# DeltaNet in a hybrid decoder trunk: half of one group's output pieces put off by an iteration, a second operand for two groups, and the late chains' steps laid anew

## The reference, cut to what matters

```python
def gated_deltanet(x, w_in, conv_w, a_log, dt_bias, out_norm_g, w_out):
    proj = x @ w_in                       # q, k, v, z and two gates per head
    qkv = silu(causal_depthwise_conv(qkv, conv_w))
    q, k = l2_normalize(q), l2_normalize(k)
    o = chunk_gated_delta_rule(q, k, v, g, beta)      # 32 heads, chunks of 64 tokens
    o = rms_norm(o, out_norm_g) * silu(z)
    return o @ w_out

def chunk_gated_delta_rule(q, k, v, g, beta):         # per head and chunk
    sol = triangular_solve(l_mat, rhs, lower=True, unit_diagonal=True)
    ...
    v_new = u_c - w_c @ state
    o_c = q_c @ state + a_c @ v_new
```

## Time and profile before

| | us |
|---|---|
| median of 3 runs | 2799.17 (2798.56 to 2801.68) |
| the profiled execution | 2803.94 |
| its span, first to last instruction | 2802.1 |
| TensorE busy | 2739.6 |
| VectorE busy | 2219.6 |
| ScalarE busy | 1648.4 |

### The profile page before, as it was taken

The page is one execution under the profiler, slowest core; times in us unless marked ns, Lnnn a source line. Parts: engine busy times, 40 slices in busy tenths (PEclk is TensorE's granted clock), DMA queues, the critical chain, the costliest instruction groups (busy, mean ns, idle before and its releaser), DMA issues.

```text
span 2802.1 us, 40252 instructions
## 1 busy us (share of the span) xinstructions
PE 2739.6 (98%) x13456; PEld 2282.1 (81%) x13456; DVE 2219.6 (79%) x2727; ACT 1648.4 (59%) x2184; POOL 31.0 (1%) x30
## 2 busy tenths in 40 slices
PE   8999999999988999999999999999999999999998
PEld 6878888888877888888888888888887888888887
DVE  5867877878767788888888876557677888888887
ACT  6766767667665555555555555554555555555554
POOL 0000000000000000000000000000000000000000
PEclk9999999999999999999999999999999999999999
DMA  6534444445433566656666656643345666656664
GB/s 239 181 124 153 159 144 163 156 149 167 158 105 113 166 210 199 198 185 203 198 198 203 198 172 224 222 135 114 106 158 188 207 199 200 199 184 200 198 201 166
DMA packets 135097, 493.23 MB, mean 176 GB/s; under 512 B 15009, under 2 KB 15329, under 8 KB 134625
## 3 DMA queue, kind: packets, MB, share of 16 engines
q1 hardware_dynamic: 133776, 487.82, 52.8%
q10 hardware_dynamic: 1232, 4.23, 0.4%
HBM read 489.86 MB, written 2.13 MB: 176 GB/s over the span
## 4 chain that ended last, share of the span: by engine, by line
PE 65%; issue 29%; DVE 3%; ACT 2%; DMA 1%; POOL 0%; POOLq 0%; DVEq 0%; SPq 0%; ACTq 0%
PE ACC L733 10%; PE ACC L735 10%; PE ACC L734 10%; PE SIDE L943 7%; PE SIDE L944 7%; PE SIDE L945 7%; PE ACC L943 3%; PE ACC L944 3%; PE ACC L945 3%; PE SIDE L741 2%; DVE W_LO L1627 1%; DMA RAW<-stream 1%; PE SIDE L1138 1%; ACT W_HI L1194 0%; ACT WORK L1587 0%
## 5 line engine op out<-in xcount | busy, mean ns | idle before, releaser
L1627 DVE TENSOR_TENSOR W_LO<-RAW,W_HI 128x1024 fp32r<-128x1024 f32 x424 | 511.6, 1222 | 268.9 <-ACT W_HI L1194 265.8
L1194 ACT ACTIVATE W_HI<-RAW 128x1024 fp32r<-128x1024 f32 x424 | 443.3, 1057 | 217.5 <-PE ACC L735 183.8
L1436 ACT ACTIVATE W_HI<-WORK 128x1024 fp32r<-128x1024 f32 x320 | 325.4, 1031 | 345.8 <-PE SIDE L945 232.7
L733 PE MATMUL ACC<-W_HI,X_HI 128*128 128x512 f32 x1216 | 491.2, 404 | 17.7 <-DVE W_LO L1627 17.6
L735 PE MATMUL ACC<-W_HI,X_LO 128*128 128x512 f32 x1216 | 477.6, 393 | 0.0
L734 PE MATMUL ACC<-W_LO,X_HI 128*128 128x512 f32 x1216 | 476.7, 392 | 0.0
L1878 DVE TENSOR_TENSOR W_LO<-WORK,W_HI 128x1024 fp32r<-128x1024 f32 x300 | 364.5, 1221 | 119.0 <-ACT W_HI L1436 116.3
L1436 ACT ACTIVATE W_HI<-RAW 128x1024 fp32r<-128x1024 f32 x328 | 314.8, 980 | 237.0 <-PE ACC L735 141.6
L733 PE MATMUL ACC<-W_HI,A_HI 128*128 128x512 f32 x928 | 370.3, 399 | 0.7 <-issue 0.7
L735 PE MATMUL ACC<-W_HI,A_LO 128*128 128x512 f32 x928 | 362.7, 391 | 0.0
L734 PE MATMUL ACC<-W_LO,A_HI 128*128 128x512 f32 x928 | 362.2, 390 | 0.0
(11 more groups left out here) (363 smaller groups left out, 3798.7 us busy)
## 6 DMA issues: line engine op xcount, KB each, us to landing
RAW<-stream SPq DMA_DIRECT2D x752, 512.0 KB, 4.6
WORK<-stream SPq DMA_DIRECT2D x160, 512.0 KB, 4.8
WORK<-gdn_rows ACTq DMA_DIRECT2D x8, 512.0 KB, 6.2
WORK<-xt SPq DMA_DIRECT2D x4, 512.0 KB, 9.3
H<-x SPq DMA_DIRECT2D x2, 1024.0 KB, 13.6
out<-WORK SPq DMA_DIRECT2D x4, 512.0 KB, 3.5
WORK<-tails SPq DMA_DIRECT2D x2, 512.0 KB, 10.8
WORK<-gfin SPq DMA_DIRECT2D x1, 1024.0 KB, 6.6
```

Source lines behind the costliest of these rows:

```text
L733: nc.tensor.matmul(dst, hi[:, at:at + P], wh, start=first and h % 2 == 0 and q == 0, stop=False)
L1194: nc.scalar.activation(W_HI[:, h % WS, :], raw_piece(h), ACT.Copy).then_inc(hi_ready, 1)
L1436: nc.scalar.activation(dst, src, ACT.Copy).then_inc(hi_ready, 1)
L1627: nc.vector.tensor_tensor(W_LO[:, h % WS, :], raw_piece(h), W_HI[:, h % WS, :].bitcast(f32), SUB).then_inc(lo_ready, 1)
```

## The change

Iteration 6 (`EDGE`) leaves the loop body and is written out with the same steps but its own list of pieces: of group 4's eight out pieces it keeps four, in slots 18, 20, 26 and 28, and z moves to 16, 17, 21, 22, 24, 25, 29 and 30. Slots 19, 23, 27 and 31 are left without a piece. The other four are done as `old4` in iteration 7 in slots 16, 18, 20 and 22, where the four pieces of group 5's out move to 23, 25, 27 and 30 and v becomes eight pieces in a row. In iteration 7 v0, s, ks, v1 and o go to slots 20, 21, 22, 23 and 25, osum and oscale to 25 and 26. In iteration 8 z and the first out pieces move a slot or more ahead, and `LAST_STEPS` puts nearly every step into a slot of its own. Groups 5 and 7 use `B_HI` and `B_LO` in place of group 6, because group 4's `A_HI` and `A_LO` are now read one iteration longer.

```diff
+EDGE = LATE_Z - 1
+OWN = (0, 1, EDGE, LATE_Z, GROUPS, GROUPS + 1)
-PIECES_7 = "qk 0 1 2 3 4 5 6 7 v 8 9 10 11 12 13 14 16 out 18 20 25 30"
-PIECES_8 = "old4 0 1 2 3 z 4 5 6 8 9 10 11 12 out 13 14 15 16 18 19 20 26"
+PIECES_6 = "qk 0 1 2 3 4 5 6 7 v 8 9 10 11 12 13 14 15 z 16 17 21 22 24 25 29 30 out 18 20 26 28"
+PIECES_7 = "qk 0 1 2 3 4 5 6 7 v 8 9 10 11 12 13 14 15 old4 16 18 20 22 out 23 25 27 30"
+PIECES_8 = "old4 0 1 2 3 z 4 5 6 7 8 9 10 11 out 12 13 14 15 16 18 19 26"
@@ def gdn_acc(it, part, n):
-    return ACCS.get((it, part, n), 0) if isinstance(it, int) and it in GDN_PIECES else GDN_ACC.get(part, 0)
+    return ACCS.get((it, part, n), 0) if isinstance(it, int) and it in GDN_PIECES and it != EDGE else GDN_ACC.get(part, 0)
@@ LAST_STEPS = gdn_table(SOLVE, """
-    0 y0 t0 u0 conv_v0a
-    2 y1 t1 u1 conv_v0b
-    3 y2 strict
-    4 t2 u2 conv_v1a
+    0 y0
+    1 t0 u0 conv_v0a
+    2 y1 conv_v0b
+    3 t1 u1
+    4 y2 strict conv_v1a
+    5 t2 u2 conv_v1b
     6 y3
-    7 t3 u3 conv_v1b silu_v
+    7 t3 u3 silu_v
     8 y4
     9 t4 u4
     10 v_t2 y5
     11 t5
     12 u5 nw
     13 ru
-    14 v0 s
-    15 ks
-    16 v1 o
-    18 osum oscale
+    14 v0
+    15 s
+    16 ks
+    17 v1
+    18 o osum
+    19 oscale
     20 o_t""")
@@ SOLVE_7 = gdn_table(SOLVE, """
     18 ru
-    19 v0
-    21 s ks
-    23 v1 fill o
-    24 osum
-    25 oscale
+    20 v0
+    21 s
+    22 ks
+    23 v1 fill
+    25 o osum
+    26 oscale
     30 o_t""")
@@ def gdn_steps(it, hs):
-    table = {0: FIRST_STEPS, 1: SOLVE_1 + PREP_1, LATE_Z: SOLVE_7 + PREP_7, GROUPS: LAST_STEPS,
+    table = {0: FIRST_STEPS, 1: SOLVE_1 + PREP_1, EDGE: SOLVE_STEPS + PREP_STEPS, LATE_Z: SOLVE_7 + PREP_7, GROUPS: LAST_STEPS,
@@ def gdn_act(g):
-            return (B_HI, B_LO) if isinstance(g, int) and g == GROUPS - 2 else (A_HI, A_LO)
+            return (B_HI, B_LO) if isinstance(g, int) and g in (EDGE - 1, LATE_Z) else (A_HI, A_LO)
@@ def gdn_scalar(act, it):
-            a_part = "old" if isinstance(it, int) and it == GROUPS else "out"
+            a_part = "old" if isinstance(it, int) and it in (LATE_Z, GROUPS) else "out"
...
-            if isinstance(it, int) and it == LATE_Z:
+            if isinstance(it, int) and it == EDGE:
                 a_free = c
@@ def _(pe):
-            with pe.Fori(2, LATE_Z) as it:
+            with pe.Fori(2, EDGE) as it:
                 gdn_tensor(pe, it)
+            gdn_tensor(pe, EDGE)
             gdn_tensor(pe, LATE_Z)
```

More of the change, by code:

```diff
@@ L112 @@
 LATE_Z = GROUPS - 1
+EDGE = LATE_Z - 1
+OWN = (0, 1, EDGE, LATE_Z, GROUPS, GROUPS + 1)
 PIECES_0 = "qk 0 1 2 3 4 6 7 8 v 9 10 11 12 13 14 15 16 z 17 18 20 21 23 25 27 29"
 PIECES_1 = "qk 0 1 2 3 4 5 6 7 v 8 9 10 11 12 13 14 15 z 16 18 20 22 25 28 29 30"
-PIECES_7 = "qk 0 1 2 3 4 5 6 7 v 8 9 10 11 12 13 14 16 out 18 20 25 30"
-PIECES_8 = "old4 0 1 2 3 z 4 5 6 8 9 10 11 12 out 13 14 15 16 18 19 20 26"
+PIECES_6 = "qk 0 1 2 3 4 5 6 7 v 8 9 10 11 12 13 14 15 z 16 17 21 22 24 25 29 30 out 18 20 26 28"
+PIECES_7 = "qk 0 1 2 3 4 5 6 7 v 8 9 10 11 12 13 14 15 old4 16 18 20 22 out 23 25 27 30"
+PIECES_8 = "old4 0 1 2 3 z 4 5 6 7 8 9 10 11 out 12 13 14 15 16 18 19 26"
 PIECES_9 = "out 0 1 2 3 4 5 6 7"
-GDN_PIECES = {0: PIECES_0, 1: PIECES_1, LATE_Z: PIECES_7, GROUPS: PIECES_8, GROUPS + 1: PIECES_9}
+GDN_PIECES = {0: PIECES_0, 1: PIECES_1, EDGE: PIECES_6, LATE_Z: PIECES_7, GROUPS: PIECES_8, GROUPS + 1: PIECES_9}
 def gdn_slots(it):
@@ L137, in gdn_accs @@
     accs, turn = {}, 0
-    for it in sorted(GDN_PIECES):
+    for it in sorted(it for it in GDN_PIECES if it != EDGE):
         slots = gdn_slots(it)
@@ L434, in gdn_uses @@
     uses, slots = [], gdn_slots(it)
-    key = it if it in (0, 1, LATE_Z, GROUPS, GROUPS + 1) else None
+    key = it if it in OWN else None
     for hs in range(32):
@@ L490 @@
 ZERO = {"a0": 0, "a1": 0, "x0": 0, "x1": 0}
-GDN = Phase(ZERO, {i: gdn_uses(i) for i in (0, 1, LATE_Z, GROUPS, GROUPS + 1)}, 2, LATE_Z, gdn_uses(2))
+GDN = Phase(ZERO, {i: gdn_uses(i) for i in OWN}, 2, EDGE, gdn_uses(2))
 NORM1 = Phase(GDN.end, {0: NORM_USES})
@@ L2288, in _ @@
             gdn_scalar(act, 1)
-            with act.Fori(2, LATE_Z) as it:
+            with act.Fori(2, EDGE) as it:
                 gdn_scalar(act, it)
+            gdn_scalar(act, EDGE)
             gdn_scalar(act, LATE_Z)
@@ L2324, in _ @@
             gdn_vector(dve, chain.link, 1)
-            chain.loop(2, LATE_Z, 13, lambda it: gdn_vector(dve, chain.link, it))
+            chain.loop(2, EDGE, 13, lambda it: gdn_vector(dve, chain.link, it))
+            gdn_vector(dve, chain.link, EDGE)
             gdn_vector(dve, chain.link, LATE_Z)
```

## The result

The changed kernel takes 2811.84 us (median of 6 runs, 2808.80 to 2814.57), the kernel before 2799.39 in the same session (6 runs, 2797.18 to 2803.40): a ratio of 1.0042, 95% interval 1.0029 to 1.0055. It is slower by 12.45 us; +8.3 was forecast.

What follows compares the result with a forecast made beforehand. TensorE, busy 98% of the span, was taken as the bound, so only its idle time and slow clock could move. Terms 4.9 + 1.65 - 4.65 + 5.6 + 0.8 gave +8.3 us, forecast 2807.5, 8-in-10 range 2794 to 2813.

Steps and rivals of the forecast that it cites:

- The empty slot 19: Iteration six, between ss and v0: of the removed piece's 2.72 us only 1.1 come back, 1.6 lost.
- qk0 2.6: End of iteration six: the next qk waits 2.6 us until ScalarE has taken z out of accumulator 1.
- s was given 2.7: Iteration seven: s, directly behind v0, idles 2.7 us for v0's copy, and the clock falls, 1.65.
- The four waits that were to go: Iteration seven: v0's 2.3 us, v1's 1.9 and the shorter ones before ks and o vanish by a piece in between.
- The step on o_t: Iteration seven: kkqk and a split precede oscale on VectorE, 11.3 us against TensorE's 7.2, so o_t stands 4.2.
- A fall of the clock there is absorbed: Iteration seven, at o_t: a fall costs nothing, since iteration eight's y0 needs masks that VectorE makes after oscale.
- the fall behind qk0 that the sum charges: First pieces of qk behind z's stripes: the clock falls, charged 1.65 us.
- o_t was given 5.3: Iteration eight's tail: o in slot 18 leaves one piece behind it, so o_t waits 5.3 us for oscale.
- waits of 2.2, 0.5, 2.2 and 1.0 with two falls of the clock: Iteration eight's four levels of y and t steps: 9.2 us in all, against 9.9 before, a gain of 0.7.
- One: Faster: fewer splits let ScalarE and VectorE run ahead; z out in time, iteration eight's level waits vanish: 2794.0 us, chance 0.16.
- Two: The clock does not fall in the new places: +4.2 us, 2803.4, chance 0.26.
- Three: Slower: VectorE 3 us later in iteration six moves o_t, z's stripe and qk, with a fall: 2811.8 us, chance 0.12.

Runs made afterwards that it cites:

- e3: The changed kernel with iteration seven's first accumulator turned, so qk0 uses the one z does not hold: 2809.19 us.
- e9: The changed kernel with old iteration eight, qk0 on the other accumulator, decay behind v0, and iteration seven's oscale a slot earlier, ahead of kkqk: 2798.92 us.
- e12: The kernel before, unaltered, run again for a second profiled execution: 2798.80 us.
- e11: The changed kernel, unaltered, run again for a second profiled execution: 2810.69 us.
- e5: The changed kernel with iteration eight's silu_v one slot later, behind y4 and ahead of t4: 2810.85 us.
- e4: The changed kernel with iteration eight's tail of steps (v0 to o_t) put back as before, its new upper levels and pieces kept: 2810.86 us.
- e8: The changed kernel with iteration eight's tail and list of pieces both put back, only its new upper levels kept: 2803.34 us.
- e10: The changed kernel with old iteration eight, qk0 on the other accumulator, decay behind v0, iteration seven's o in slot 24 and oscale in 25: 2795.19 us.
- e1: The kernel before with only iteration eight's new table of steps and list of pieces: 2808.64 us.

## Why the prediction was right in direction, and 4 us short

**Iteration six: right in each step.** The empty slot 19 was given 1.6: v0 idles 1.2, and from ru to s it takes 7.88 us instead of 8.99, so that 1.6 of the piece's 2.72 are lost. o was given 0.8 and idles 0.8, qk0 2.6 and idles 2.1 (2.4 from start to start, e3). ScalarE's table load in front of the stripes cost its 1.28 and no more, as the sum took it: the extra 1.38 of draining that the Trainium skill gives ("ScalarE: Activation LUTs", "What ACT_TABLE_LOAD costs") would have made the 2.6 into 4.0, and decay's exponential starts 0.01 behind its load as well (805.36 + 1.28, then 806.65).

**Iteration seven: right in sum, one cause half seen.** s was given 2.7 and idles 2.5, with the clock down behind it; o_t 4.2 and 3.9; nw 0.9 and 0.9; ru 0.8 and 1.0. The four waits that were to go are gone. The step on o_t named oscale alone; e9 shows a second holder, kkqk's bank, that ends only 3.5 us earlier (L1782, the same reader, ends at 838.00 in the changed kernel, oscale at 841.52) and becomes the last as soon as oscale is put in front. "A fall of the clock there is absorbed" was wrong: from its start to the next piece's o_t took 1.59 instead of 0.79, and the piece behind it was slow too; the masks that were to hide this were through at 845.27, y0 started at 846.92. The kernel before had shown L1774 as the last there (at e9, above). That the stretch came within 0.3 is partly luck, since it hangs on two executions: the fall behind qk0 that the sum charges came in three of seven, and the kernel before had two falls in iteration seven that e12 has not. With e11 and e12 as the pair seven is +8.6, six -5.9 and eight +9.4; eight's miss stays.

**Iteration eight: o_t and v1 right, t4 and the clock wrong.** o_t was given 5.3 and idles 5.2, v1 1.9 and 1.9, ru 0.7 more than before and idles 0.9 more (1.7, before 0.8). What failed is "waits of 2.2, 0.5, 2.2 and 1.0 with two falls of the clock": t1 and t3 idle 2.0 each and no fall followed, but t4 idles 2.2 and did have one, t2 idles 0.8 instead of 0.5, and two shorter waits (0.5 and 0.2, at y3 and y1) came on top. The levels idle 7.7 us where the walk had 5.9. It had left out silu_v's 2.35 on ScalarE in front of y4's copy, though e5 shows that a slot later costs the same; no run takes silu_v out of the levels.

The missing 3.7 are 1.6 of idle time and 2.1 of slow work. TensorE idles 16.45 us in iteration eight, before 9.28: 7.2 more, where the sum has 5.6 more; the levels overshoot it by 2.3 and the rest falls 0.7 short. It is busy 79.35, before 76.42: 2.9 more, where the sum has 0.8. Of this, the levels had one fall instead of the two charged (1.6 less), v1 a whole one where half was charged (0.8 more), and 2.0 are slow work around the two o_ts, charged at nothing: eight's own o_t takes 1.59 instead of 0.79, the piece behind it 3.60 instead of 3.01, and the first piece of iteration eight, behind seven's o_t, 3.66 instead of 3.09. The last 0.9 is spread over many steps and pieces.

**Rivals.** One (the engines run ahead) is refuted: the t steps, o_t and qk0 wait as walked. Two (no falls in new places) is half true: t1 and t3 went free, and qk0's went free in four of seven executions; s, t4 and mostly v1 did not. Three gives the right time, 2811.8, for a wrong reason: iteration six's o_t doesn't wait at all. The measured 2811.84 lies inside the forecast's own range only at its very edge, 2812.

## What to carry to other kernels

A filler piece taken from behind a long chain (o, root, oscale) and put where it parts two steps cost 5.15 us here (e4 against e8): it took 2.8 off the wait in front of which it was put, two later waits grew by as much together, and o_t waits 4.0 behind the chain. Look also at what a piece brings with it: where the addition to H fell inside the chain, one more piece covered 1.2 us of the wait, not the 2.7 that TensorE spends on it; the split fell beside ScalarE's square and cost nothing. Before reordering what stands on the last engine's queue, look for the second holder: the operand and the bank, as at o_t, can both be that engine's work, and then what helped was to start the whole chain earlier (e10). A trace of the kernel before may show that holder already. Charge a fall of the clock behind a wait as a chance, not as a price, and look at more than one execution before a difference of 2 us between two traces is given a cause.

## What the runs showed of the hardware

Whether TensorE's clock falls from 2.4 to 1.2 GHz for some of the next piece isn't decided by the length of the wait in front alone. By the granted clock of the first 3 to 4 us behind it, over the executions in which the same wait stood in the same place: s in iteration seven (2.5 us idle) fell in 7 of 7; t4 (2.2) in 4 of 4; v1 in iteration eight (1.9) in 4 of 6; qk0 (2.1) in 3 of 7; t3 (2.0) in 2 of 7; t1 (2.0) in 1 of 8. With the old iteration seven (both executions of the kernel before, and e1), v0's 2.3 was followed by a fall in 1 of 3 and v1's 1.9 in 2 of 3. Two of these rows are qk0's above, 0.62 and 1.00 behind the same idle time. What differs between such executions the profile doesn't show. The Trainium skill, "TensorE: Matmul & The Clock Gate", section "HAM oscillation — how this bites in real kernels", would let gaps this short do no harm; t1 and t3 mostly agree with it, s and t4 never do.

Behind the long waits of o_t, 3.9 to 5.2 us, the clock was down within o_t's own eight transposes in 17 of 17 cases: they took 1.5 to 1.6 us up to the next piece's start instead of 0.8.

GpSimd's root on 128x8 took 1.64 us in iteration seven of the changed kernel and 2.54 in iterations six and eight (the column of POOL above), with the same shape. It goes by what VectorE is doing as the root starts. In all 14 profiled executions it took 1.63 or 1.64 where that was an instruction with an accumulator or a bank as one input (kkqk's L1777 in the changed kernel; in e10 the addition to H), ten cases, and 2.54 to 2.75 where it was a split or oscale's first half, which read neither, 102 cases. e9, with oscale's first half in kkqk's place, has 2.54. That one causes the other is not shown; no run was made for it.
